# Last attention head: high halves of the seven finished heads' outputs made on GpSimd behind their reload

## What is computed

```
p = softmax(q k / 8 + bias)          # two maps per head, 8 heads, 8 blocks of 128 queries
a = p[:, :, 0] - lam * p[:, :, 1]
o = a v                              # per head, 1024 x 128
o = rmsnorm(o, subln) * (1.0 - lam_init)
return o.reshape(bsz, s, H * 2 * dh) @ w_o
```

## Time and profile before

| | |
|---|---|
| median of 3 runs | 2930.65 us |
| lowest and highest run | 2929.97 and 2932.02 us |
| span of the profiled execution | 2927.1 us (no time of its own is given beside it) |
| what the runs have over that span | 2.9 to 4.9 us, median 3.55 us |
| PE, DVE, ACT, POOL busy | 97%, 66%, 40%, 15% of the span |

### The profile page before, as it was taken

One profiled execution on the slowest core, in us unless ns is written; L12 is line 12 of the kernel. 1 busy time (PEld: TensorE's weight loads), 2 busy tenths in 40 slices (PEclk: granted clock), 3 DMA queues, 4 the chain that ended last, 5 costly groups with the idle time before them and its releaser, 6 DMA issues.

```text
span 2927.1 us, 34428 instructions
## 1 busy us (share of the span) xinstructions
PE 2844.0 (97%) x13489; PEld 2265.7 (77%) x13489; DVE 1921.0 (66%) x2492; ACT 1161.9 (40%) x1708; POOL 442.2 (15%) x323
## 2 busy tenths in 40 slices
PE   8999999999999999999999999999799999999999
PEld 6767778767778888877767888888676888887887
DVE  6548866656587666765667766776737866666254
ACT  2223325213343333433245565556624433334342
POOL 0420011360004332202000000000000232222020
PEclk7999999999999999999999999999999999999999
DMA  6344475025132222375540111111133222226453
GB/s 216 110 136 151 145 224 194 29 79 201 54 131 80 75 86 87 124 251 183 176 157 18 47 43 43 43 43 45 64 101 101 87 86 87 87 65 203 136 158 116
DMA packets 361686, 326.60 MB, mean 112 GB/s; under 512 B 11501, under 2 KB 319182, under 8 KB 361486
## 3 DMA queue, kind: packets, MB, share of 16 engines
q1 hardware_dynamic: 348486, 271.61, 29.7%
q0 software_dynamic: 12000, 48.61, 4.5%
q10 hardware_dynamic: 1040, 4.19, 0.4%
HBM read 263.88 MB, written 68.35 MB: 114 GB/s over the span
## 4 chain that ended last, share of the span: by engine, by line
PE 90%; DVE 5%; ACT 2%; DMA 1%; issue 1%; POOL 1%; SPq 0%; ACTq 0%; DVEq 0%; POOLq 0%
PE psum_gemm L1953 20%; PE psum_misc L1953 18%; PE psum_gemm L2399 8%; PE psum_gemm L216 6%; PE psum_gemm L217 6%; PE psum_gemm L220 6%; PE psum_misc L2463 3%; PE psum_gemm L2484 3%; PE psum_gemm L2472 3%; PE psum_gemm L318 2%; PE psum_misc L216 2%; PE psum_misc L217 2%; PE psum_misc L220 2%; PE psum_misc L888 1%; PE psum_gemm L2485 1%
## 5 line engine op out<-in xcount | busy, mean ns | idle before, releaser
L216 PE MATMUL psum_gemm<-h_hi,w_hi 128*128 128x512 f32 x816 | 329.3, 404 | 12.0 <-DVE h_lo L401 8.2
L217 PE MATMUL psum_gemm<-h_lo,w_hi 128*128 128x512 f32 x816 | 318.5, 390 | 0.0
L198 ACT ACTIVATE w_hi<-w_raw 128x1024 fp32r<-128x1024 f32 x93 | 97.8, 1055 | 455.1 <-PE psum_gemm L220 321.4
L1878 DVE TENSOR_TENSOR ring_lo<-piece_raw,ring_hi 128x512 fp32r<-128x512 f32 x192 | 137.0, 722 | 206.2 <-ACT ring_hi L1872 205.7
L220 PE MATMUL psum_gemm<-h_hi,w_lo 128*128 128x512 f32 x816 | 251.9, 390 | 0.0
L203 DVE TENSOR_TENSOR w_lo<-w_raw,w_hi 128x1024 fp32r<-128x1024 f32 x93 | 119.1, 1285 | 158.5 <-ACT w_hi L198 158.5
L1872 ACT ACTIVATE ring_hi<-piece_raw 128x512 fp32r<-128x512 f32 x192 | 112.7, 593 | 246.2 <-PE psum_misc L1953 208.3
L1953 PE MATMUL psum_misc<-h_hi,ring_hi 128*128 128x512 f32 x512 | 200.6, 392 | 0.6 <-DVE ring_lo L1878 0.6
L216 PEld LDWEIGHTS psum_gemm<-h_hi,w_hi 128*128 128x128 f32 x816 | 153.2, 188 | 61.5 <-issue 20.8
L1953 PE MATMUL psum_misc<-h_hi,ring_lo 128*128 128x512 f32 x512 | 199.4, 389 | 0.0
L1953 PE MATMUL psum_misc<-h_lo,ring_hi 128*128 128x512 f32 x512 | 199.2, 389 | 0.0
(11 more groups left out here) (422 smaller groups left out, 6792.3 us busy)
## 6 DMA issues: line engine op xcount, KB each, us to landing
ada_w<-in_w_ada SPq DMA_DIRECT2D x28, 1024.0 KB, 5.5
w_raw<-in_f_w_up SPq DMA_DIRECT2D x52, 512.0 KB, 4.9
ffn_act_scratch<-gate_act SPq DMA_DIRECT2D x42, 512.0 KB, 2.6
piece_raw<-in_f_w_down SPq DMA_DIRECT2D x80, 256.0 KB, 3.2
piece_raw<-ffn_act_scratch SPq DMA_DIRECT2D x80, 256.0 KB, 2.9
pair_raw<-in_f_w_up SPq DMA_DIRECT2D x36, 512.0 KB, 5.1
w_raw<-in_e_w_in SPq DMA_DIRECT2D x29, 512.0 KB, 4.5
x_scratch<-x_res SPq DMA_DIRECT2D x3, 4096.0 KB, 12.6
```

The costliest lines, as they stand in the source:

```text
L198: act.activation(w_hi[:, s], w_raw[:, s], ACT.Copy).then_inc(s_hi, 1)
L216: pe.matmul(o, wh, rh[:, k, c], start=(k == 0), stop=False)
L217: pe.matmul(o, wh, rl[:, k, c], start=False, stop=False)
L1878: dve.tensor_tensor(Al[:, idx % 7, 0:n], src, Ah[:, idx % 7, 0:n].bitcast(F32), ALU.subtract).then_inc(s_wl, 1)
```

## The change

The seven copies leave ScalarE's program and stand in GpSimd's, right after the issue of the reload of head 6 and ahead of the scaling of head 7. The line numbers behind the edit are two lower than before.

```diff
                 if g >= CH and g % CH == O_STEP:
                     o_copy(g // CH - 1)
-                if g > NB - CH:
-                    o_hi(act, g - NB + CH - 1)
             o_square(NB - 2)
...
-        def o_hi(act, k):
+        def o_hi(pool, k):
 
-            act.wait_ge(s_ord[k == 6], 16)
-            act.activation(Hh[:, k], o_raw[:, k], ACT.Copy).then_inc(s_oh, 1)
+            pool.wait_ge(s_ord[k == 6], 16)
+            pool.tensor_copy(Hh[:, k], o_raw[:, k]).then_inc(s_oh, 1)
...
                 if h == 6:
                     pool.wait_ge(s_os, 112)
                     pool.dma_start(o_raw[:, 6], o_dram[6]).then_inc(s_ord[1], 16)
+                    for k in range(LAST):
+                        o_hi(pool, k)
```

## The result

The changed kernel takes 2939.35 us (median of 6 runs, 2934.62 to 2948.73) against 2931.34 us for the kernel before (6 runs, 2929.97 to 2933.78): ratio 1.0026, 95% interval 1.0016 to 1.0037. It is slower, by 8.0 us in the medians (0.3%), and the forecast of 2931.5 us with its range up to 2934.3 us was wrong.

The account below looks back on a forecast made before the run. The last head was taken as an engine-to-engine chain: 1.4 us of VectorE waits less 0.16 us from the removal, +0.9 us after the clock. Span 2927.1 gives 2928.0, plus 3.55 to the median: 2931.5 us, range 2929.0 to 2934.3.

Parts of the forecast that it names:

- What bounds the kernel, and the removal: Last head is a chain from engine to engine; removing 7.3 us of ScalarE copies takes about 0.16 us off it.
- the rival that ScalarE was the bound: All seven copies of 1.047 us come back, giving 2923.3 us; chance 0.01.
- What the addition costs GpSimd: Seven casts of 1.04 us ahead of head 7's scaling end at about 2104, before their first user; cost 0.
- casts at a two-input rate: Casts take 1.92 us each, so ratio and combine wait longer: +2.6 us, 2933.3 us; chance 0.07.
- GpSimd as the bound: Casts push head 7's scaling behind TensorE's need for it: 2937 us and more; chance 0.02.
- What it costs VectorE: VectorE and GpSimd take turns: combine(62) costs 0, ratio and combine of block 63 cost 1.4 us; net +1.2 us.
- The ends are 0 and 2.0 us; I take 1.4: Delay at block 63, where ratio or combine waits for running casts and one cast may go ahead.
- 0.2 us before the first cast can: combine(62) starts at 2094.38, ahead of the first cast, which waits about 1.0 us; cost to VectorE 0.
- Rival 2: The first cast gets ahead of combine(62), so both combines are caught: another 1.0 us, 2932.5 us; chance 0.10.
- TensorE's clock: Slow stretch from 2101.0 to 2104.8 may stay in place and return up to 0.6 us; +0.9 us taken.
- Rival 4: Longer wait before transposes(63) adds or removes a 1.2 GHz stretch of 1.6 us: 2933.1 or 2929.9 us; chance 0.13, equally divided.

Follow-up runs that it names:

- one column per cast: Changed kernel with GpSimd casting only one column of each of the seven tiles: 2931.17 against 2932.24 us for the kernel before, ratio 0.9998.
- four casts: Changed kernel with heads 0 to 2 copied by ScalarE again, heads 3 to 6 cast by GpSimd: 2936.04 us, ratio 1.0024 to the kernel before.
- one gap: Changed kernel with one wait added, the fifth cast waiting for the fourth to be complete: one run of 2932.51 us.
- the change, TensorE kept busy: Changed kernel plus 36 matmuls into an unused bank ahead of block 62's transposes: 2936.80 us, beside 2938.59 us for the changed kernel.
- two-input operations: Changed kernel with each cast replaced by a two-input GpSimd product with 1: 2944.95 against 2929.34 us for the kernel before, ratio 1.0049.

## Why the prediction was wrong

**What bounds the kernel, and the removal: right.** The seven copies were hidden but for 0.16 us; the run with one column per cast measured 0.14 us at a_hi(62), and the rival that ScalarE was the bound fell.

**What the addition costs GpSimd: right.** 1.033 us per cast against 1.04 and no cost at the scaling of head 7. The end at 2103.5 against "about 2104" is partly luck: the casts started 2.0 us later than reckoned, and the waits that the text allowed for did not come. The rivals of casts at a two-input rate and of GpSimd as the bound fell with it.

**What it costs VectorE: wrong, and this step decides.** "So one waits until the other's instruction is over, and they take turns" was read from one collision in layer 0 and carried over to seven instructions in a row. In this series, which has no open wait, no turn is given. With turns (a wait between the casts) the longest ratio is 1.52 us; without them 7.39 us in two profiles and 7.41 in a third. The term "The ends are 0 and 2.0 us; I take 1.4" measured 7.2 us, and all of it at block 62, which the text had at 0; at block 63, which the term was for, nothing waited. Its upper end was set by one cast per VectorE instruction instead of by the series, 6.93 us. Why turns were taken in layer 0 and not here stays open.

**The first user was overlooked.** For block 62 the text costed the combine, at 2094.38, as "0.2 us before the first cast can", and left out the ratio ahead of it. In the changed kernel that ratio starts 0.45 us before the first cast's record and is kept out all the same; with the ratio out of the way the combine was kept out from 0.13 us before it. A margin of tenths of a microsecond against a full cast's record was no cover. What gives one engine the first turn stays open, since with casts of one column a margin of 0.19 us did cover the combine. Rival 2 had this place and, by the same rule of turns, a price of 1.0 us.

The Trainium skill (SBUF — State Buffer, Who interferes with whom) names two conditions for this contention: two SBUF inputs on VectorE, and a GpSimd instruction that reads SBUF rather than only writing it. These runs agree: the one-input ratio passed in 0.27 us, and the memsets held up nothing. A one-element input counted too. The Trainium skill (SBUF — State Buffer, SBUF: two separate sides) has the first to start hold the shared pair of ports "for the whole instruction"; here VectorE waited for seven, and the measurement decides.

**TensorE's clock: wrong in sign.** The text let the fixed low stretch give back up to 0.6 us. After 9.40 us of idle time the 1.2 GHz level held for 22.5 us, and between transposes(62) and o_lo(0) it cost 3.2 us. Rival 4 had the sign in its bad half, with one stretch of 1.6 us. But no single sign would have been right for every stall. How late each place comes against the kernel before, counted from the save, in us:

| run | transposes(62) | o_lo(0) | difference |
|---|---|---|---|
| a wait between the casts | 1.8 at transposes(63), behind its second wait | 4.2 | +2.4 |
| four casts | 4.0 | 3.1 | -0.9 |
| one gap | 4.2 | 3.4 | -0.8 |
| ratio with one input | 6.9 | 10.1 | +3.2 |
| the change | 7.2 | 10.3 | +3.2 |
| the change, TensorE kept busy | 7.2 | 6.9 | -0.3 |
| two-input operations | 13.3 | 14.1 | +0.8 |

With four casts and with one gap the granted clock is back at 1.00 from 14 us behind the save on, after about 7 us at the low level that began in the idle time, and the prediction's idea that some time comes back holds. In the changed kernel the low level goes on until 34.6 us behind the save. Of the 10.3 us lost by o_lo(0) the whole run keeps 8.0 us in the first medians and 6.4 in the second; in the two profiles 9.97 us are left at the end. (The time of most executions lies 1.7 to 1.8 us above their span, so the profiled one of the kernel before took some 2928.9 us, an estimate, 2.4 us under the median, and the changed kernel's lies 1.5 us over its own.) Low stretches in other parts differ between executions too, which is as far as the difference was followed.

## To carry to other kernels

Work moved to GpSimd in one block that reads SBUF can stop a VectorE instruction with two SBUF inputs for the length of the block, so the price to write down as the bad case is that length, against the chain, however small VectorE's instruction is. Either put the block where VectorE has no two-SBUF-input instruction due, or give it real waits between its instructions; then VectorE's wait was one cast at most. A stall on a chain that TensorE is part of moves the stretches of low clock behind it as well. Here that was worth between -0.9 and +3.2 us, and the length of the stall did not tell which.

## What the runs showed that was not expected

- VectorE's wait follows the series: 6.93 us of casts gave 7.39 us, 12.99 us of products 13.47 us, one gap after four casts 4.44 us, a gap after each 1.52 us.
- It begins up to 0.47 us ahead of the record of the first operation of 1024 columns on GpSimd; memsets in the same place gave none, and ahead of casts of one column neither the ratio (0.44 us) nor the combine (0.19 us) was held.
- TensorE stayed at 0.50 for 22.5 us, though it was busy for 7.15 of the first 7.9 us and for 7.05 of the next 10.0; it came back to 0.99 behind 4.6 us in which it was busy for 4.54.
- In layer 0 VectorE got its turn between two GpSimd operations with no open wait between them, which these experiments don't explain.
